# A two-layer decoder trunk on one core: layer 1's query norm, rotary weights, key scaling, first output product and order of loads changed

## What is computed

```python
c_q = rms_norm(h @ w_dq, q_latent_norm)
q = (c_q @ w_uq).reshape(B, S, 16, 96)
q = rms_norm(q, q_norm)                       # over the 96 entries of a head
q = concat([q[..., :64], apply_rope(q[..., 64:], pos)])
# k likewise, from the shared latent: k_nope per head, k_pe shared by the heads
s = einsum(q, k) * 96 ** -0.5                 # causal mask
p = softmax(s)
y = einsum(p, v).reshape(B, S, 1024) @ w_o
x = x + gate * y
```

## Time and profile before

| | us |
|---|---|
| median of three runs | 1338.48 (1336.87 to 1340.49) |
| the profiled execution, its own time | 1336.37 |
| span of its trace | 1334.6 |
| PE busy | 1102.6 |
| DVE busy | 439.1 |
| ACT busy | 252.9 |
| POOL busy | 0.4 |

### The profile page before, as it was taken

How to read it: one execution, slowest core, us unless ns; L and a number is a source line. 1 busy time by engine, 2 the same in 40 slices (tenths; PEclk the granted TensorE clock), 3 DMA queues, 4 the chain that set the end, 5 groups by cost and what they waited for, 6 DMA issues and landing times.

```text
span 1334.6 us, 17222 instructions
## 1 busy us (share of the span) xinstructions
PE 1102.6 (83%) x6664; PEld 613.9 (46%) x6664; DVE 439.1 (33%) x1028; ACT 252.9 (19%) x572; POOL 0.4 (0%) x5
## 2 busy tenths in 40 slices
PE   5999899998787778877679889999868888867776
PEld 4886477454233323333237468745323333423332
DVE  1297765221112112111137866622111212111213
ACT  1122613111101111011022372311011101110100
POOL 0000000000000000000000000000000000000000
PEclk9998999999889899889889999999889989988988
DMA  9996979999999999999986756589999999999994
GB/s 349 385 405 276 368 287 362 380 425 423 423 424 425 423 423 424 424 425 422 423 329 247 284 190 245 228 351 426 422 424 424 425 423 423 424 424 424 424 424 203
DMA packets 99915, 502.26 MB, mean 376 GB/s; under 512 B 11866, under 2 KB 37367, under 8 KB 44535
## 3 DMA queue, kind: packets, MB, share of 16 engines
q1 hardware_dynamic: 99366, 500.92, 92.1%
q10 hardware_dynamic: 464, 0.20, 0.1%
HBM read 500.04 MB, written 1.05 MB: 375 GB/s over the span
## 4 chain that ended last, share of the span: by engine, by line
SPq 45%; PE 33%; DMA 9%; DVE 6%; issue 4%; ACT 2%; DVEq 0%; ACTq 0%
SPq L598 42%; PE bank L733 26%; DMA w_gu<-in_moe_w_gate_up 6%; SPq L687 3%; PE bank L1121 2%; PE bank L736 2%; DMA w_gu_x<-in_moe_w_gate_up 2%; DMA ring<-in_ada_w 2%; PE bank L956 1%; ACT p_sb L1357 1%; PE bank L1102 1%; PE bank L879 1%; DVE s_sb L1635 0%; DVE x L1854 0%; DVE y_lo L1803 0%
## 5 line engine op out<-in xcount | busy, mean ns | idle before, releaser
L733 PE MATMUL bank<-w_gu,ring 128*32 128x512 f32 (+1 forms) x1088 | 343.7, 698 | 80.3 <-DMA w_gu<-in_moe_w_gate_up 54.5
L733 PEld LDWEIGHTS bank<-w_gu,ring 128*32 128x32 f32 (+1 forms) x1088 | 90.3, 134 | 213.6 <-issue 213.6
L733 PE MATMUL bank<-ring 128*32 128x512 f32 (+1 forms) x384 | 161.5, 690 | 21.0 <-DMA w_gu<-in_moe_w_gate_up 20.8
L1786 DVE TENSOR_TENSOR hh<-sg,bank 128x256 f32<-128x256 f32 x44 | 27.4, 624 | 429.5 <-ACT sg L1388 429.5
L733 PE MATMUL bank<-w_gu_x,ring 128*32 128x512 f32 (+1 forms) x320 | 144.0, 666 | 25.9 <-DMA w_gu<-in_moe_w_gate_up 21.7
L733 PE MATMUL bank<-w_gu,hhT 128*32 128x512 f32 (+1 forms) x576 | 147.2, 599 | 1.4 <-DMA w_gu<-in_moe_w_down 1.2
L733 PE MATMUL bank<-w_dn,ring 128*32 128x512 f32 x240 | 103.8, 808 | 26.3 <-DMA w_gu<-in_moe_w_gate_up 10.7
L1803 DVE SCALAR_TENSOR_TENSOR y_lo<-bank,w_slot,y_hi 128x512 fp32r<-128x512 f32 x88 | 62.0, 746 | 174.3 <-ACT y_hi L1280 174.3
L1388 ACT ACTIVATE sg<-bank 128x256 f32<-128x256 f32 x44 | 16.9, 385 | 507.4 <-PE bank L733 507.4
L733 PE MATMUL bank<-sel,h_hi 128*128 128x256 f32 x352 | 87.7, 289 | 0.0
L733 PE MATMUL bank<-sel,h_lo 128*128 128x256 f32 x352 | 84.2, 279 | 0.0
(11 more groups left out here) (291 smaller groups left out, 1571.5 us busy)
## 6 DMA issues: line engine op xcount, KB each, us to landing
w_gu<-in_moe_w_gate_up SPq DMA_DIRECT2D x126, 1024.0 KB, 25.9
w_gu<-in_moe_w_down SPq DMA_DIRECT2D x68, 1024.0 KB, 26.3
ring<-in_moe_w_gate_up SPq DMA_DIRECT2D x44, 1024.0 KB, 26.7
w_gu_x<-in_moe_w_gate_up SPq DMA_DIRECT2D x38, 1024.0 KB, 25.2
ring<-in_ada_w SPq DMA_DIRECT2D x36, 1024.0 KB, 10.2
w_dn<-in_moe_w_gate_up SPq DMA_DIRECT2D x30, 1024.0 KB, 25.7
ring<-in_moe_w_down SPq DMA_DIRECT2D x16, 1024.0 KB, 26.1
w_dn<-in_moe_w_down SPq DMA_DIRECT2D x14, 1024.0 KB, 26.7
```

Source lines behind the costliest of these rows:

```text
L733: return nc.tensor.matmul(o, a, b, start=first, stop=last)
L1786: v.tensor_tensor(hh[:, :].rearrange("s (f p) -> s p f", f=FE // P), sg[:, :].rearrange("s (p f) -> s p f", f=FE // P), bank[b][:, FE:2 * ...
```

## The change

1. Layer 1's queries are no longer multiplied by their reciprocal norm. The reciprocals go into `rs_q`, ACT's exponential takes them as its scale (a value per partition), and `nmax` is multiplied by them on DVE.
2. The query norm's weights for the rotary part are multiplied once into four small tables `rope_q`, and the multiplication in each turn is gone.
3. The four multiplications of k go to GpSimd, which waits for the key reciprocal; PE waits for them ahead of its first transposes.
4. In both layers the first quarter of the output product is made in three pieces: four of its eight k blocks after the values of pair 5, two after those of pair 6, two after the last.
5. ACT's sines move up to its eighth piece.
6. In layer 0 SP issues four early units ahead of the last three chunks of group 6 and the fifth and sixth ahead of chunk `("ada", 3, 3)`; the chunks of the shared expert and of `dq` take other numbers, and so other slots of the ring. The order in which PE uses them stays.

The diff, cut to what follows from these points:

```diff
@@ tiles and tables
+        rs_q = sb("rs_q", [P, NT * H])
+                rope_q = in_kT(4, NT, ROPE // 2)
+        def rs_of(h, ti):
+            at = 2 * 4 * (h // 4) + 4 * ti + h % 4
+            return rs_q[:, at:at + 1]
@@ order of the chunks
                 chunk(("kvd", 1, 0), kvd[:, :, 0:KVR], KT, KVR)
+                chunk(("dq", 1, 0), dq[:, :, 0:256], KT, 256)
                 chunk(("kvd", 1, 1), kvd[:, :, KVR:KVR + ROPE], KT, ROPE)
                 chunk(("dq", 1, 1), dq[:, :, 256:QR], KT, QR - 256)
-                chunk(("dq", 1, 0), dq[:, :, 0:256], KT, 256)
...
                 wo_chunk(2)
-                ada_chunks(g, 5, KT)
-                sgu_chunks()
+                ada_chunks(g, 5, 6)
+                sgu_chunk(0)
+                ada_chunks(g, 6, KT)
+                sgu_chunk(1)
...
-        WO_BANK = (2, 3, 4, 5)
+        WO_BANK = (0, 1, 4, 5)
@@ SP's queue, layer 0
-                    load_chunks(order[9:number[("wo", 0, 1)] + 1])
+                    load_chunks(order[9:21])
                     fixed_loads(0, EARLY_UNITS[0:2])
                     sp.wait_ge(sem("qkv_ps"), 8)
                     fixed_loads(0, EARLY_UNITS[2:4])
-                    load_chunks(order[number[("ada", 3, 3)]:number[("ada", 3, 6)] + 1])
+                    load_chunks(order[21:number[("wo", 0, 1)] + 1])
                     sp.wait_ge(sem("qkv_ps"), 10)
                     fixed_loads(0, EARLY_UNITS[4:6])
-                    load_chunks([("ada", 3, 7)])
+                    load_chunks(order[number[("ada", 3, 3)]:number[("ada", 3, 5)] + 1])
+                    load_chunks([("ada", 3, 6), ("ada", 3, 7)])
@@ PE, attention (both layers)
+                def first_output(k0, k1):
+                    w = use(("wo", l, 0))
+                    for k in range(k0, k1):
+                        pe.wait_ge(sem("o_sb"), pairs + k + 1)
+                        for ti in range(NT):
+                            last = nc.tensor.matmul(bank[WO_BANK[0]][:, ti * N:(ti + 1) * N], hT[:, k, ti * P:(ti + 1) * P], w[:, k, :],
+                                                    start=k == 0 and ti == 0, stop=k == KT - 1, skip_group_check=True)
+                    if k1 == KT:
+                        used(("wo", l, 0), last)
...
                     if g >= 3:
                         values(g - 3)
-
-                pe.wait_ge(sem("o_sb"), pairs + H // 2)
-                for c in range(4):
+                    if g == H // 2:
+                        first_output(0, 4)
+                    if g == H // 2 + 1:
+                        first_output(4, 6)
+
+                first_output(6, KT)
+                for c in range(1, 4):
@@ PE, layer 1's transposes of q and k
                 pe.wait_ge(sem("qk_norm"), g // 2 + 2)
+                if g == 0:
+                    pe.wait_ge(sem("k_norm"), 4)
@@ ACT
                                 last = nc.scalar.activation(p_sb[:, h % 4, c0:c1], s_sb[:, h % 4, c0:c1], ACT.Exp,
-                                                            bias=nmax[:, h, ti:ti + 1], accum_out=lsum[:, h, ti:ti + 1])
+                                                            bias=nmax[:, h, ti:ti + 1], scale=rs_of(h, ti) if l else 1.0,
+                                                            accum_out=lsum[:, h, ti:ti + 1])
...
                 if c == 8:
                     ada_rows(1)
+                    act.wait_ge(sem("angles"), 1)
+                    for a in range(2):
+                        last = nc.scalar.activation(sincos[:, a, :, :], ang[:, 2 + a, :, :], ACT.Sin)
+                    last.then_inc(sem("sines"), 1)
...
-            act.wait_ge(sem("angles"), 1)
-            for a in range(2):
-                last = nc.scalar.activation(sincos[:, a, :, :], ang[:, 2 + a, :, :], ACT.Sin)
-            last.then_inc(sem("sines"), 1)
@@ DVE, layer 1's attention: nmax
+                            rs = rs_q[:, 8 * (g // 2):8 * (g // 2) + 8].rearrange("p (t h) -> p h t", t=NT)
+                            last = v.scalar_tensor_tensor(out=nmax[:, 2 * g:2 * g + 2, :], in0=smax[:, 2 * g:2 * g + 2, :], scalar=-1.0,
+                                                          in1=rs[:, 2 * (g % 2):2 * (g % 2) + 2, :], op0=ALU.mult, op1=ALU.mult)
@@ DVE, layer 1's rotary parts and norms
+            gain_q = ropeg[:, 0, :].rearrange("p (a r) -> p a r", a=2)
+            for n, (f, a) in enumerate(((cos, 0), (sin, 1), (sin, 0), (cos, 1))):
+                last = v.tensor_tensor(rope_q[:, n, :, :], f, gain_q[:, a:a + 1, :].broadcast_to([P, NT, half_r]), ALU.mult)
+            link(V, last)
...
-            def q_norm(j):
+            def q_scale(j):
                 dve.wait_ge(sem("qk_rt"), j + 2)
                 r = slice(8 * j, 8 * j + 8)
-                link(V, v.reciprocal(hs_row(4)[:, r], hs_row(2)[:, r]))
-                qj = q_sb[:, :, 4 * j:4 * j + 4, :]
-                v.tensor_tensor(qj, qj, hs_row(4)[:, r].rearrange("p (t h) -> p t h", t=NT).unsqueeze(3)
-                                .broadcast_to([P, NT, 4, QK]), ALU.mult).then_inc(sem("qk_norm"), 1)
...
+                v.reciprocal(rs_q[:, r], hs_row(2)[:, r])
+
+            dve.wait_ge(sem("qk_rt"), 1)
+            v.reciprocal(hs_row(5), hs_row(3)).then_inc(sem("qk_norm"), 1)
...
-                if j == 0:
-                    k_norm()
-                else:
-                    q_norm(j - 1)
+                if j:
+                    q_scale(j - 1)
...
-                pe_part = q_sb[:, :, 4 * j:4 * j + 4, HD:QK]
-                link(V, v.tensor_tensor(pe_part, pe_part, ropeg[:, 0:1, :].unsqueeze(2).broadcast_to([P, NT, 4, ROPE]), ALU.mult))
...
+                last.then_inc(sem("qk_norm"), 1)
+                dve.wait_ge(sem("qk_norm"), j + 2)
+            q_scale(3)
@@ GpSimd
+            pool.wait_ge(sem("qk_norm"), 1)
+            for ti in range(NT):
+                kn = k_sb[:, ti, :, 0:HD]
+                rs = hs_rs[:, 5, ti, :].unsqueeze(2)
+                nc.gpsimd.tensor_tensor(kn, kn, rs.broadcast_to([P, H, HD]), ALU.mult).then_inc(sem("k_norm"), 1)
+                nc.gpsimd.tensor_tensor(k_sb[:, ti, :, HD:QK], kpe[:, ti:ti + 1, :].broadcast_to([P, H, ROPE]),
+                                        rs.broadcast_to([P, H, ROPE]), ALU.mult).then_inc(sem("k_norm"), 1)
```

More of the change, by code:

```diff
@@ L448, in wo_chunk, with sgu_chunk @@
                 chunk(("wo", l, j), wo[:, :, j * 256:(j + 1) * 256], KT, 256)
-            def sgu_chunks():
-                for j in range(2):
-                    chunk(("sgu", l, j), sgu[:, :, j * 256:(j + 1) * 256], KT, 256)
+            def sgu_chunk(j):
+                chunk(("sgu", l, j), sgu[:, :, j * 256:(j + 1) * 256], KT, 256)
             g = ADA_IN_WO[l]
@@ L1638, in attention @@
                         link(V, last)
-                        v.tensor_scalar(nmax[:, 2 * g:2 * g + 2, :], smax[:, 2 * g:2 * g + 2, :], -1.0, None, ALU.mult)\
-                            .then_inc(sem("s_ready"), 2)
+                        if l == 0:
+                            last = v.tensor_scalar(nmax[:, 2 * g:2 * g + 2, :], smax[:, 2 * g:2 * g + 2, :], -1.0, None, ALU.mult)
+                        else:
+                            rs = rs_q[:, 8 * (g // 2):8 * (g // 2) + 8].rearrange("p (t h) -> p h t", t=NT)
+                            last = v.scalar_tensor_tensor(out=nmax[:, 2 * g:2 * g + 2, :], in0=smax[:, 2 * g:2 * g + 2, :], scalar=-1.0,
+                                                          in1=rs[:, 2 * (g % 2):2 * (g % 2) + 2, :], op0=ALU.mult, op1=ALU.mult)
+                        last.then_inc(sem("s_ready"), 2)
                     if g >= 1:
@@ L1698, in experts @@
                 dve.wait_ge(sem("ranks"), l + 1)
-                v.scalar_tensor_tensor(out=slot_of[:, :, :], in0=bank[4][:, 0:NT * E].rearrange("p (t e) -> p t e", t=NT),
-                                       scalar=1.0, in1=chosen[:, :, :], op0=ALU.add, op1=ALU.mult).then_inc(sem("slots"), 1)
-                dve.wait_ge(sem("slots"), l + 1)
+                link(V, v.scalar_tensor_tensor(out=slot_of[:, :, :], in0=bank[4][:, 0:NT * E].rearrange("p (t e) -> p t e", t=NT),
+                                       scalar=1.0, in1=chosen[:, :, :], op0=ALU.add, op1=ALU.mult))
                 def parts(i):
@@ L1960, in rotate @@
                      for n in range(4)]
-                for n, (m, f) in enumerate(((a, c), (b, s), (a, s), (b, c))):
+                for n, (m, f) in enumerate(zip((a, b, a, b), fs)):
                     last = v.tensor_tensor(r[n], m, f, ALU.mult)
@@ L2014, in _ @@
                                 ALU.add).then_inc(sem("qk_ss"), 1)
-                pe_part = q_sb[:, :, 4 * j:4 * j + 4, HD:QK]
-                link(V, v.tensor_tensor(pe_part, pe_part, ropeg[:, 0:1, :].unsqueeze(2).broadcast_to([P, NT, 4, ROPE]), ALU.mult))
-                rotate(q_sb[:, :, 4 * j:4 * j + 4, HD:HD + half_r], q_sb[:, :, 4 * j:4 * j + 4, HD + half_r:QK],
```

(8 more changed lines are left out.)

15 lines of the change are left out of this document (3 added, 12 removed).

## The result

The changed kernel takes 1343.89 us, median of 15 runs (1338.99 to 1349.12). The kernel before takes 1340.46 over 15 runs (1336.87 to 1345.57); the three runs shown ahead of the prediction had it at 1338.48. The ratio is 1.0035, 95% interval 1.0021 to 1.0049. So the change made the kernel slower by 3 to 7 us. The prediction said 1331.0 (1326 to 1337.5) and gave "slower" a chance of 0.08.

What follows compares the result with a forecast made beforehand. Bound by bytes (423 GB/s) in the expert streams, by the PE, DVE and ACT chain in attention. Layer 0's 4.9 + layer 1's 2.6 = 7.5 off 1336.37: 1328.9; median 2.1 above, so 1331 (1326 to 1337.5).

Steps and rivals of the forecast that it cites:

- reaches the end in full: Attention parts: a microsecond off the compute chain starts the weight stream a microsecond earlier, same bytes left, all of it kept.
- layer 1's part: All terms of layer 1's attention: 4.6 - 2.5 + 0.9 + 1.0 - 1.4, 2.6 us of gain.
- Query loop with GpSimd: Layer 1: fewer DVE multiplications in the query loop gain 4.6 us; GpSimd's key multiplications delay DVE by 2.5.
- rival of full alternation: Layer 1: each GpSimd instruction blocks DVE once, delay 4.9 us; layer 1 gives -1.4, total 1335; chance 0.18.
- Exponential's scale: Layer 1: 20 exponentials on the chain each take 0.07 us longer with a scale per partition; loss 1.4 us.
- Output product: Both layers: begun early, it removes PE's waits of 0.57 and 0.47 us for ACT's copies; gain 1.0 per layer.
- Order of loads: Layer 0: early units fill a DMA gap; the last ada chunk delays the last quarter's add less; gain 1.4 us.
- Sines: Layer 0: at ACT's piece eight they cost nothing, ending PE's 1.13 us idle before the modulation row; gain 1.1.
- Layer 0's clock: Layer 0: with a 1.6 us wait gone, norm products take 3.84 us as in layer 1, not 5.46; gain 1.4.
- Layer 1's clock at the transposes: Layer 1, 760 to 780 us: PE's idle 2.01 us shrinks, less work at the lower clock; gain 0.9.
- The scale is free: Rival, layer 1: the exponential's scale costs nothing; 1.4 us more gain, 1329.5; chance 0.05.
- The reordered loads bring nothing: Rival, layer 0: the last chunk still comes late; 2.8 us less gain, 1334; chance 0.06.

Runs made afterwards that it cites:

- e1_shift: Kernel before plus an unused tile of 128 bytes per partition where the change declares rs_q, no instruction changed: 1347.80 us, ratio 1.0059.
- e3: Kernel before with only the change's order of loads and ring chunks (both layers' lists, SP's order in layer 0): 1339.10 us, ratio 0.9991.
- e5: Kernel before with an unused tile of 128 bytes per partition ahead of every other tile: 1331.2 us, ratio 0.9925.
- e7: Kernel before with unused tiles of 128 bytes ahead of all tiles and where the change declares rs_q: 1330.60 us, ratio 0.9925.
- e11: Kernel before with 384 unused bytes per partition ahead of all tiles: 1332.7 us, ratio 0.9927.
- e12: Kernel before with 64 unused bytes per partition ahead of all tiles: 1347.4 us, ratio 1.0045.
- e13: The kernel of e7 run again, on the same chip and in the same call as e14 and e15: 1333.27 us, ratio 0.9944 to the kernel before.
- e2: Changed kernel with rs_q declared behind layer 1's attention tiles, so every other tile lies where the kernel before had it: 1338.07 us, ratio 0.998.
- e6: Changed kernel with an unused tile of 128 bytes ahead of every other tile: 1333.54 us, ratio 0.9935 to the kernel before.
- e14: The kernel of e6 run again, on the same chip and in the same call as e13 and e15: 1329.56 us, ratio 0.9920 to the kernel before.
- e4: Changed kernel with the four key multiplications on DVE in the query loop's first turn, not on GpSimd: 1343.23 us, ratio 1.0018 to the kernel before.
- e15: The kernel of e9 run again, on the same chip and in the same call as e13 and e14: 1328.81 us, ratio 0.9913 to the kernel before.
- e10: The kernel of e7 with layer 1's exponential taking a scale of ones from SBUF: 1337.00 us, ratio 0.9961 to the kernel before.
- e8: The kernel of e7 plus the change's sines, loads, output product and linked slots; layer 1's norms and exponential as before: 1331.21 us, ratio 0.9920.
- e9: The kernel of e6 with key multiplications on DVE and their reciprocal behind the first q copy: 1326.59 us, ratio 0.9891 to the kernel before.

## Why the prediction was wrong

**The step that failed is one that has no term.** The prediction said that a microsecond off the chain "reaches the end in full", since the streams move the same bytes at 423 GB/s. The change declares `rs_q` ahead of most tiles. That moved w_gu_1 from a multiple of 256 bytes to 128 past one; its packets lost their 309 ns, those of the other targets grew too, both streams ran at 421 GB/s and cost 2.7 and 4.9 us more. e1_shift prices it at 7.5 us (1347.80 - 1340.29 of the kernel before beside it), as much as the whole forecast gain. The prediction did call itself wrong "if the streams' lengths change". That was the right place to look, and nothing was worked out for it.

**A second step failed: layer 1's part, forecast as 2.6 us of gain.** From DVE's load of the table behind layer 0's stream to the cast of layer 1's table, before's code takes 175.3 to 176.6 us in eight traces (before, e1, e3, e5, e7, e11, e12, e13), and the changed code 177.1 to 178.6 in all four (after, e2, e6, e14), some 2.2 more. Layer 0's part up to its table is 220.4 to 227.4 in eight traces of before's code there, 224.9 in the middle, and 219.7 to 221.7 in eight of the change's, 220.5 in the middle: a gain of 4.4. The two give 2.2 net, near what e2 and e14 measured. The terms below say where layer 1's forecast gain went.

**The base.** The sum was set against a profiled execution of 1336.37 and a median of three. The median of 15 lies 4.1 above that execution, not 2.1. The execution had no slow piece of clock in layer 0's output product (granted clock 1.00 from 160 to 170 us, where e1 and e11 have 0.83): last scores to last quarter took 31.0 us, and in eight other traces of the same code there 32.3 to 33.6. Two of the missing microseconds are no effect of the change.

**The terms one by one.** I read each from the traces of all kernels with the same code in that stretch. A slow piece is a stretch at the lower level of the clock, 1.2 GHz. Cuts of layer 1, in us (DVE's first q copy, first v copy, first and last score row, last product with `gate`, last scaling of hT, each by its start; e11 and e12 are as the first column up to the last product):

| stretch | before, e1, e5, e13 | e3, e7 | after | e2, e6 | e14 | e4 | e15 | e10 | e8 | e9 |
|---|---|---|---|---|---|---|---|---|---|---|
| q copy to v copy | 21.3 | 21.3 | 18.60 | 20.3 | 18.61 | 17.85 | 18.33 | 21.26 | 21.26 | 18.31 |
| to first scores | 12.9 | 11.3 | 11.55 | 11.56 | 11.55 | 11.56 | 11.55 | 12.87 | 11.29 | 11.56 |
| to last scores | 22.9 | 24.5 | 25.92 | 25.9 | 25.91 | 24.34 | 24.35 | 25.97 | 26.08 | 27.14 |
| to last residual | 36.35 | 36.35 | 35.78 | 35.8 | 35.78 | 35.77 | 35.78 | 36.72 | 37.05 | 37.39 |
| to last hT | 6.64 | 9.18, 8.01 | 9.18 | 6.64 | 7.97 | 6.64 | 6.63 | 6.64 | 8.18 | 8.26 |

- Query loop with GpSimd: forecast 4.6 - 2.5 = 2.1. Measured 21.26 - 18.60 = 2.66, less 0.74 because the loop starts that much later: the stretch ahead of it, from DVE's copy of `kpe`, is 25.08 in eight traces of the old order and 25.82 in after, e4 and e14. The keys' reciprocal and its wait now stand ahead of the first q copy (740.81, idle 0.39, above). Net 1.9, in after and e14. It isn't what every trace has: that stretch is 26.3 in before and e9, 27.9 in e8 and 28.6 to 28.7 in e2 and e6, whose loop takes 20.3 besides, so in e2 and e6 nothing is gained by the time of the v copy. The 0.74 was an unlisted moved step; e15 has it back. GpSimd's delay was taken as 2.5 and is 4.04 - 0.90 = 3.1: the rival of full alternation had the mechanism right.
- Exponential's scale: forecast -1.4. Stretches without a slow piece are 22.92 and 24.34, 1.42. Right in size for the operand; e10_scale shows the 93 ns alone. What the forecast left out: of the eight traces with the operand six (after, e2, e6, e14, e10, e9) have some 1.6 or more of slow clock in this stretch, and only e4 and e15 have none.
- Output product: forecast 1.0 per layer. 36.35 to 35.78 is 0.6 in layer 1. In layer 0 (last scores to the last quarter's product) the usual 32.5 falls to 31.7, and the shortest, 31.0, to 30.1: 0.8 to 0.9.
- Order of loads: forecast 1.4. From that product to the add of its result 8.53 falls to 7.18 in after and e2, 1.35; against aligned kernels of before's code (8.3) it is 1.1.
- Sines: forecast 1.1. The idle 1.13 is gone, but PE then waits 0.48 for DVE's modulation step. Layer 0's score stretch at its shortest is 30.1 (e5) and 30.2 (e7) with before's code and 29.3 to 29.8 in six traces with the change's: some 0.6. With a slow piece it is 32.5 to 32.6 in five traces of the one and 32.4 in e14, so it may be less.
- Layer 0's clock: forecast 1.4, measured 0 against the trace of before. The norm products still take 5.46 (in other traces of before's code they take 5.2 to 6.7, in all of the change's 5.3 to 5.5). I had put the slow clock down to the wait of 1.6, and PE still idles 1.21 and 0.53 ahead of them without it:

```profile
192.71 1.04 PE L742 MATMUL bank<-acc,cst 128*1 128x512 f32 x8
194.96 1.05 PE L742 MATMUL bank<-cst,kT 128*128 128x4 f32 x8 [1.21 <-DVE kT L1619]
196.54 5.46 PE L742 MATMUL bank<-xn,x 128*128 128x128 f32 x32 [0.53 <-DVE xn L1610]
```

- Layer 1's clock at the transposes: forecast 0.9. Against the trace of before it is 12.92 - 11.55 = 1.4, but it was given back in the next stretch. The table shows it: before's code has 12.9 + 22.9 or 11.3 + 24.5, 35.8 in all eight traces. One slow piece, in one place or the other. The changed code has 11.55 + 25.9 = 37.5 in its four traces, the operand's 1.4 and 0.3 more; only with the keys on DVE, in e4 and e15, is it 35.9, with no slow piece in either. The windows 760 to 780 and 780 to 800 us (PEclk third from the end) of e13_before_aligned and of after:

```profile
760.00:780.00 20.00, 17.06 (x110) 12.57 (x109) 14.17 (x46) 11.09 (x29) 0.00 (x0) 0.91 0.58 224
780.00:800.00 20.00, 15.25 (x127) 11.29 (x125) 13.63 (x79) 16.50 (x64) 0.00 (x0) 1.00 0.25 93
```

```profile
760.00:780.00 20.00, 16.94 (x119) 13.23 (x117) 14.93 (x58) 14.92 (x38) 0.00 (x0) 1.00 0.74 282
780.00:800.00 20.00, 15.86 (x122) 12.09 (x122) 11.13 (x62) 16.03 (x56) 0.00 (x0) 0.91 0.11 36
```

PE's rows in after name the spot. It idles 2.55 us for ACT's copy, then the same eight score matmuls that take 1.48 ahead of it and 1.58 later take 2.34, partly at the level of 1.2 GHz; e4 has the same wait of 2.55 there and stays at 2.4 GHz, so the wait doesn't decide it alone:

```profile
776.67 1.48 PE L742 MATMUL bank<-kT,qT 96*128 96x128 f32 x8
780.70 1.02 PE L745 MATMUL bank<-cst,p_sb 128*128 128x128 f32 x6 [2.55 <-ACT pT_sb L1306]
...
783.13 2.34 PE L742 MATMUL bank<-kT,qT 96*128 96x128 f32 x8
...
786.86 1.58 PE L742 MATMUL bank<-kT,qT 96*128 96x128 f32 x8
```

In sum, without the clock terms: 0.6 + 0.8 + 1.2 in layer 0, and 1.9 + 0.6 - 1.4 - 0.3 in layer 1 (the 0.3 is 11.29 to 11.55 at the transposes). That is 3.4, and e14 against e13 measures 3.2. The agreement is in part luck: the 0.8 for layer 1 is what stretches without a slow piece give, and no trace of the changed code is free of one in layer 1, where all four took 1 to 3 us more than the middle of before's code; layer 0, against before's other traces, gained more than 2.6. The forecast's 7.5 was those 3.4, plus 2.3 of clock that didn't stay, and 1.8 of small excess. By this estimate the miss of 12.9 us (1343.9 - 1331.0) is 4.1 of terms, 7.5 of place and 2.0 of base, 0.7 too much.

**The rivals.** Alternation was the right mechanism and cost 0.6 more than the forecast's own term (3.1 against 2.5), not the 4.9 of delay written for it, since GpSimd was faster. Whether its price in clock belongs to it stays open: with the keys on DVE layer 1 takes 173.5 and 173.2 us in e4 and e15, but 178.5 in e9. "The scale is free" is wrong by e10_scale. "The reordered loads bring nothing" is wrong by the traces. None of the rivals had the address.

**Open.** Which executions have a slow piece at layer 1's norm products (3.84, or 5.2 to 6.8 us) or in the query loop (18.6 or 20.3) isn't settled: it differs between executions of the same code (after, e2, e6, e14), e3 has it with the loads alone, and no run here controls it. That e15 beats e14 is seen in its stretches (25.08 and 18.33 against 25.82 and 18.61), not in its time; e9, the same code, has 26.34 and 18.31. Why an offset of w_gu_1 alone costs nothing is open too.

## What to carry to other kernels

Before trusting "same bytes, same rate", work out where each DMA target starts when a tile is added, and try the large ones at multiples of 256 bytes: here one unused tile of 128 bytes ahead of the others took 10 us off a kernel of 1340 that moves 500 MB, more than all the reordering together. Cost every declaration as an edit, and compare variants only at equal addresses. A gain by the clock in one stretch counts only if the next stretches show that it isn't given back.

## What the runs showed of the hardware

- 8 KB packets from HBM into SBUF take 309 ns where the large targets start at multiples of 256 bytes, w_gu_1 on one (e7) or not (e5, e11), and 314 where no target does (e1, e12). The core's rate is 426 to 427 GB/s in the first case, 421 in the second, and 423 to 424 with w_gu_1 alone on a multiple (before, e2, e3).
- GpSimd multiplies 128x1024 floats in 1.90 to 1.95 us and 128x512 in 1.05 to 1.09, where DVE takes 1.21 to 1.23 and 0.68. Beside it four DVE products of two SBUF inputs took 4.04 us in place of 0.89, a reduction of one input 0.95 as ever.
- A second operand from SBUF lengthens an exponential by 93 ns.
